# Sample attention in groups of four sequences on four column groups

## The reference, cut to what matters

```python
# prompt, per head: causal softmax over 256 positions
s_own = jnp.einsum('qhd,khd->qhk', q, k_own) * ATTN_SCALE
# sample, per sequence: 4 queries against 256 cached keys and its own new ones
kseq = jnp.concatenate([pool_k[pages].reshape(past, h, dh), kn, zeros], axis=0)
vseq = jnp.concatenate([pool_v[pages].reshape(past, h, dh), vn, zeros], axis=0)
# layer B: three groups (window, dilation) (128,1), (512,4), (2048,16), then
w = jax.nn.softmax(jnp.stack(lses, axis=0), axis=0)
o = jnp.sum(w[..., None] * jnp.stack(outs, axis=0), axis=0)
```

## Time and profile before

| | us |
|---|---|
| median of 3 runs (1825.51 to 1825.96) | 1825.53 |
| the profiled execution | 1829.23 |
| its span, first to last instruction | 1827.2 |
| attention A, 126.5 to 262.7 | 136.2 |
| attention B, 611.3 to 710.2 | 98.9 |

### The profile page before, as it was taken

One profiled execution on the slowest core, in us unless ns is written; L12 is line 12 of the kernel. 1 busy time (PEld: TensorE's weight loads), 2 busy tenths in 40 slices (PEclk: granted clock), 3 DMA queues, 4 the chain that ended last, 5 costly groups with the idle time before them and its releaser, 6 DMA issues.

```text
span 1827.2 us, 24864 instructions
## 1 busy us (share of the span) xinstructions
PE 1735.5 (95%) x9086; PEld 1434.3 (78%) x9086; DVE 1362.0 (75%) x1721; ACT 1038.8 (57%) x1043; POOL 56.1 (3%) x81
## 2 busy tenths in 40 slices
PE   7999989999989898589999999999999999999998
PEld 6876779999978677477877877877878878878776
DVE  5863426655577683788898888897888888988987
ACT  5433324443354241456776766776767767767765
POOL 0001101000000110100000000000000000000000
PEclk9998869999999897599999999999999999999999
DMA  9345414544643420188998998998998989989985
GB/s 327 116 154 175 139 46 135 165 141 122 201 156 116 141 105 24 47 277 321 362 336 326 356 344 321 359 334 328 354 346 324 355 312 361 345 322 360 335 326 200
DMA packets 232981, 452.97 MB, mean 248 GB/s; under 512 B 7584, under 2 KB 79264, under 8 KB 232784
## 3 DMA queue, kind: packets, MB, share of 16 engines
q1 hardware_dynamic: 224656, 421.93, 65.6%
q0 software_dynamic: 8256, 30.12, 5.0%
HBM read 447.30 MB, written 4.72 MB: 247 GB/s over the span
## 4 chain that ended last, share of the span: by engine, by line
PE 86%; DVE 8%; ACT 3%; issue 1%; DMA 1%; DVEq 0%; POOLq 0%; SPq 0%; ACTq 0%
PE psum L241 23%; PE psum L243 23%; PE psum L242 23%; PE psum L538 3%; PE psum L599 3%; PE psum L753 2%; PE psum L737 2%; DVE wlo L237 1%; PE psum L773 1%; PE psum L555 1%; ACT whi L233 1%; PE psum L580 1%; DVE rs L1150 1%; PE psum L521 1%; PE psum L476 1%
## 5 line engine op out<-in xcount | busy, mean ns | idle before, releaser
L237 DVE TENSOR_TENSOR wlo<-raw,whi 128x2048 fp32r<-128x2048 f32 (+1 forms) x404 | 911.5, 2261 | 227.6 <-ACT whi L233 227.5
L233 ACT ACTIVATE whi<-raw 128x2048 fp32r<-128x2048 f32 (+1 forms) x404 | 764.9, 1896 | 321.6 <-PE psum L243 321.5
L241 PE MATMUL psum<-whi,xgh 128*128 128x512 f32 x896 | 360.4, 402 | 7.7 <-DVE wlo L237 6.3
L243 PE MATMUL psum<-whi,xgl 128*128 128x512 f32 x896 | 356.4, 398 | 0.0
L242 PE MATMUL psum<-wlo,xgh 128*128 128x512 f32 x896 | 354.7, 396 | 0.0
L241 PE MATMUL psum<-hh,whi 128*128 128x288 f32 x800 | 246.1, 308 | 14.0 <-DVE hl L1294 9.1
L243 PE MATMUL psum<-hh,wlo 128*128 128x288 f32 x800 | 240.0, 300 | 0.0
L242 PE MATMUL psum<-hl,whi 128*128 128x288 f32 x800 | 239.1, 299 | 0.0
L241 PEld LDWEIGHTS psum<-whi,xgh 128*128 128x128 f32 x896 | 169.4, 189 | 49.0 <-DVE wlo L237 6.7
L243 PEld LDWEIGHTS psum<-whi,xgl 128*128 128x128 f32 x896 | 169.2, 189 | 41.2
L242 PEld LDWEIGHTS psum<-wlo,xgh 128*128 128x128 f32 x896 | 169.5, 189 | 39.6
(11 more groups left out here) (293 smaller groups left out, 1776.3 us busy)
## 6 DMA issues: line engine op xcount, KB each, us to landing
raw<-in_w_gu_moe SPq DMA_DIRECT2D x226, 1024.0 KB, 5.1
raw<-in_w_down_moe SPq DMA_DIRECT2D x112, 1024.0 KB, 5.0
raw<-in_w_gu_dense SPq DMA_DIRECT2D x22, 1024.0 KB, 5.1
raw<-in_w_qkv_a SPq DMA_DIRECT2D x12, 1024.0 KB, 12.5
raw<-in_w_down_dense SPq DMA_DIRECT2D x16, 704.0 KB, 4.6
kraw_a<-in_cache_a_k POOLq DMA_DIRECT2D x16, 512.0 KB, 4.6
vraw_a<-in_cache_a_v POOLq DMA_DIRECT2D x16, 512.0 KB, 4.9
raw<-in_w_q_b SPq DMA_DIRECT2D x6, 1024.0 KB, 5.1
```

The lines of the kernel that those rows point to most:

```text
L233: nc.scalar.activation(whi[:, p % SPL, 0:size], raw[:, p % RAW, 0:size], ACT.Copy).then_inc(hi_ready, 1)
L237: nc.vector.tensor_tensor(wlo[:, p % SPL, 0:size], raw[:, p % RAW, 0:size], whi[:, p % SPL, 0:size].bitcast(F32), ALU.subtract).then_inc(p ...
L241: nc.tensor.matmul(out, lh, rh, start=start, stop=False)
L243: return nc.tensor.matmul(out, ll, rh, start=False, stop=stop)
```

## The change

Each layer's attention becomes ten jobs in the order `JOBS`: eight prompt units ("p") and two groups of four sample sequences ("s"), and three more steps to finish. The transposes of the cached keys are laid out over the steps by `FILLS` (which sequences' keys in which step).

- Scores of a group: for each sequence and each of the four column groups, one matmul with 32 stationary columns (a pair of heads, 8 real columns in a band that belongs to that sequence) writes 32 rows of a tile of 128 rows (4 pairs x 4 sequences x 2 heads x 4 queries). Four sequences accumulate into one tile. In A there are two tiles (two groups of four pairs), in B one for each dilation group.
- Softmax: the maximum, `exp` and the sum run over a whole tile of 128 rows. The division by the sum comes after the values, as a scale of ACT's copy (`scale_out`).
- Values: the transposed probabilities (32 columns) are stationary and 128 value columns move; the new tokens come first, as one matmul of 512 moving columns for each pair. Of the 128x512 result, the diagonal blocks are wanted: `pick_rows` gets them by matmuls with slices of the identity, between `scale_out` (ACT) and `sample_out` (DVE).
- Loads: keys come one page at a time into a ring of 3 (A) or 6 (B) pages; transposed keys have 2 (A) or 4 (B) places. The values still have two places, and the load for sequence `q` waits for `spv_done` of `q - 2`.
- Gone: `sample_scores`, `turn_sample`, the old `sample_values` and L628.

Cut to its core (the lines that are left out are the matching buffers, masks, the DVE list and the removed code):

```diff
+JOBS = [("p", 0), ("p", 1), ("p", 2), ("s", 0), ("p", 3), ("p", 4), ("p", 5), ("p", 6), ("s", 1), ("p", 7)]
+FILLS = [(0,), (1, 2), (3,), (4,), (5,), (), (), (6, 7)]
...
+            def value_pages(b, q):
+                tg = b["tag"]
+                if q >= 2:
+                    eng.wait_ge(sem(f"spv_done_{tg}"), q - 1)
+                if b is A:
+                    for j in range(2):
+                        pg = eng.value_load(pgt[0:1, 2 * q + j:2 * q + j + 1], min_val=0, max_val=NPHYS - 1)
+                        eng.dma_start(b["vraw"][:, q % 2, j, :], io["cache_a_v"][0][bass.ds(pg, 1), :, :].rearrange("a p n -> p (a n)"))\
+                            .then_inc(sem(f"vraw_loaded_{tg}{q % 2}"), 16)
+                else:
+                    eng.dma_start(b["vraw"][:, q % 2], io["cache_b_v"][q].rearrange("(j p) n -> p j n", p=P)).then_inc(sem(f"vraw_loaded_{tg}{q % 2}"), 32)
...
+            def caches(b, first):
+                for pgi in range(first, 6):
+                    key_page(b, pgi)
+                eng.wait_ge(sem(f"kv_stored_{b['tag']}"), 64)
+                value_pages(b, 0)
+                value_pages(b, 1)
+                for pgi in range(6, 12):
+                    key_page(b, pgi)
+                for q in (2, 3):
+                    value_pages(b, q)
+                for pgi in range(12, 16):
+                    key_page(b, pgi)
+                for q in range(4, NSEQ):
+                    value_pages(b, q)
...
+                def sample_scores_a(q):
+                    keys_ready(q)
+                    if q == 4:
+                        eng.wait_ge(sem(f"so_copied_{tg}"), hp)
+                    s = q % 4
+                    for x in range(hp):
+                        for c in range(4):
+                            j = 4 * x + c
+                            ins = nc.tensor.matmul(ps[sbank + x][32 * c:32 * c + 32, 0:T], b["qblk"][:, s * b["qrow"] + 32 * j:s * b["qrow"] + 32 * j + 32],
+                                                   b["keys"][:, q % b["kb"], j, :], start=s == 0, stop=s == 3)
                     ins.then_inc(sem(f"sscored_{tg}"), 1)
...
+                def sample_scores_b(k, gr):
+                    eng.wait_ge(sem(f"exped_{tg}"), exped_count(b, k - 1))
+                    keys_ready(4 * gr + 3)
+                    for g in range(ng):
+                        for s in range(4):
+                            for c in range(nj):
+                                at_ = (4 * g + s) * b["qrow"] + 32 * c
+                                ins = nc.tensor.matmul(ps[b["score_banks"][g]][32 * c:32 * c + 32, 0:T], b["qblk"][:, at_:at_ + 32],
+                                                       b["keys"][:, s, c, :], start=s == 0, stop=s == 3)
+                        ins.then_inc(sem(f"sscored_{tg}"), 1)
...
+                def sample_values(k, gr):
+                    eng.wait_ge(sem(f"pt_copied_{tg}"), (k + 1) * hp)
+                    if ng > 1 and gr == 1:
+                        eng.wait_ge(sem(f"so_copied_{tg}"), hp)
+                    for x in range(hp):
+                        for c in range(4):
+                            new = b["vtok"][0:NSAMP, 2, (4 * x + c) * P:(4 * x + c + 1) * P].unsqueeze(1).to_broadcast([NSAMP, 4, P])
+                            nc.tensor.matmul(ps[sbank + x][32 * c:32 * c + 32, :].rearrange("p (s n) -> p s n", s=4),
+                                             b["spt"][0:NSAMP, x, 2 * P + 32 * c:2 * P + 32 * c + 32], new, start=True, stop=False)
+                    for s in range(4):
+                        q = 4 * gr + s
+                        eng.wait_ge(sem(f"vraw_loaded_{tg}{q % 2}"), 32 * (q // 2 + 1))
+                        for x in range(hp):
+                            for half in range(2):
+                                for c in range(4):
+                                    j = 4 * x + c
+                                    ins = nc.tensor.matmul(ps[sbank + x][32 * c:32 * c + 32, s * P:(s + 1) * P],
+                                                           b["spt"][:, x, half * P + 32 * c:half * P + 32 * c + 32],
+                                                           b["vraw"][:, q % 2, half, j * P:(j + 1) * P], start=False, stop=s == 3 and half == 1)
+                        ins.then_inc(sem(f"spv_done_{tg}"), 1)
...
+                def pick_rows(gr, x):
+                    eng.wait_ge(sem(f"so_scaled_{tg}"), gr * hp + x + 1)
+                    for s in range(4):
+                        for r in range(2):
+                            ins = nc.tensor.matmul(ps[sbank + x][64 * r:64 * r + 64, 16 * s:16 * s + 16], b["pvs"][:, s * P + 64 * r:s * P + 64 * r + 64],
+                                                   pick[:, s, r], start=True, stop=True)
+                    ins.then_inc(sem(f"picked_{tg}"), 1)
...
+                for t in range(len(JOBS) + 3):
+                    fills = slot_fills(b, t)
+                    kind, u = JOBS[t] if t < len(JOBS) else ("", 0)
+                    done, du = JOBS[t - 1] if 1 <= t <= len(JOBS) else ("", 0)
+                    if kind == "p":
+                        scores(t, u)
+                    elif kind == "s" and ng > 1:
+                        sample_scores_b(t, u)
+                    for n in fills[0:2]:
+                        turn_keys(n)
+                    if done:
+                        turn_probs(t - 1, 0)
+                    if ng == 1:
+                        for q in ((), (0,), (1,), (2, 3), (), (), (), (4, 5), (6, 7))[t] if t < 9 else ():
+                            sample_scores_a(q)
+                    for n in fills[2:]:
+                        turn_keys(n)
+                    if done and hp == 2:
+                        turn_probs(t - 1, 1)
+                    if t >= 2 and t - 2 < len(JOBS) and JOBS[t - 2][0] == "s":
+                        sample_values(t - 2, JOBS[t - 2][1])
+                    if done == "p":
+                        values(t - 1, du)
+                    if t >= 3 and t - 3 < len(JOBS) and JOBS[t - 3][0] == "s":
+                        for x in range(hp):
+                            pick_rows(JOBS[t - 3][1], x)
...
+                def scale_out(gr, x):
+                    eng.wait_ge(sem(f"spv_done_{tg}"), 4 * (gr + 1))
+                    if x == 1:
+                        eng.wait_ge(sem(f"picked_{tg}"), gr * hp + 1)
+                    nc.scalar.activation(b["pvs"][:, :], ps[b["s_bank"] + x][:, :], ACT.Copy, scale=b["sst"][:, gr, 8 + x:9 + x])\
+                        .then_inc(sem(f"so_scaled_{tg}"), 1)
...
+                for t in range(len(JOBS) + 3):
+                    fills = [n for n in slot_fills(b, t) if n % 2 == 0]
+                    done, du = JOBS[t - 1] if 1 <= t <= len(JOBS) else ("", 0)
+                    for n in fills[0:1]:
+                        copy_keys(n)
+                    if done:
+                        copy_probs(t - 1, 0)
+                    for n in fills[1:]:
+                        copy_keys(n)
+                    if t < len(JOBS):
                         for x in range(hp):
+                            exp(t, x)
+                    if done and hp == 2:
+                        copy_probs(t - 1, 1)
+                    if done == "p" and (du * hp + hp - 1) % 2 == 1:
+                        h = du * hp + hp - 1
+                        eng.wait_ge(sem(f"pv_done_{tg}"), du + 1)
+                        nc.scalar.activation(b["oT"][:, h // 2, 0:SEQ], ps[b["pv_bank"]][:, 0:SEQ], ACT.Copy).then_inc(sem(f"o_copied_{tg}"), 1)
+                    if t >= 3 and t - 3 < len(JOBS) and JOBS[t - 3][0] == "s":
+                        for x in range(hp):
+                            scale_out(JOBS[t - 3][1], x)
...
```

More of the change, by code:

```diff
@@ L160, in build_program, with slot_fills @@
+        def slot_fills(b, t):
+            return [n for q in (FILLS[t] if t < len(FILLS) else ()) for n in range(2 * b["fills"] * q, 2 * b["fills"] * (q + 1))]
         A["dest"] = [A["qT"][:, i] for i in range(8)] + [A["kT"][:, i] for i in range(8)]
@@ L387, in norm_add @@
+            for pgi in range(3):
+                key_page(A, pgi)
+            store(A, io["ak"], io["av"])
+            caches(A, 3)
             def norm_add(tag, before):
@@ L651, in _ @@
             to_tokens(A)
[L652 removed]
+            attend(A)
             residual(P_WO, tiles_wo, KD, "wo", "o_split_a", hh2, hl2)
@@ L1164, in attend @@
             def attend(b):
-                tg, nj, ng, hp, kr, hq, rows = b["tag"], b["nj"], b["ng"], b["hp"], b["kr"], b["hq"], b["rows"]
-                two = len(b["kt_banks"]) == 2
-                chain(V.memset(b["qblk"][:, :, :], 0.0))
-                V.tensor_copy(b["keys"][:, :, PAST:PAST + NSAMP], b["kT"][:, :, SEQ:T]).then_inc(sem(f"new_keys_{tg}"), 1)
+                tg, nj, ng, hp = b["tag"], b["nj"], b["ng"], b["hp"]
+                for i in range(b["kb"]):
+                    ins = V.tensor_copy(b["keys"][:, i, :, PAST:T], b["kT"][:, :, SEQ:T])
```

(35 more changed lines are left out.)

447 lines of the change are left out of this document (166 added, 281 removed).

## The result

The changed kernel took 1832.47 us (median of five, 1831.77 to 1834.65), the kernel before 1825.51: ratio 1.0042, 95% interval 1.0029 to 1.0056. Compared once more later, with twelve executions, it was 1.0018 [1.0004, 1.0032]. So it is slower, by 0.2 to 0.4%; the forecast was 1829.5, which is 4.0 above the kernel before, and the two comparisons have 7.0 and 3.5 by their medians. The profiled execution took 1832.47 with a span of 1830.8, against 1827.2 before.

The account below looks back on a forecast made before the run. The prediction took PE to bound the kernel (86% of the span ends on it). A gaining 7.3 us and B losing 11 gave net +4: profiled 1829.2 becomes 1833, less 3.7 to the median, 1829.5; range 1809 to 1843.

Parts of the forecast that it names:

- What goes from PE: PE in both attentions: sets of four column-group matmuls replace sample scores and values; A's PE falls from 127 to about 65 us.
- slot walk: Both attentions, durations summed slot by slot from the first exp to the split: A 122.4 us, B 100.4 us.
- Rival 3: Column groups' weight loads in both attentions don't overlap running matmuls: +10 us, 1839; chance 0.06.
- The loop between the engines: Prompt slots of both attentions: scores, maximum, exp, probabilities and handovers take 6.1 us a slot, 7.3 or 7 at half clock.
- The value waits: Each group's third sequence's values load late; PE waits about 6 then 1.5 us in A, 4 in B, twice per layer.
- The slots: Eleven slots in each attention, priced one by one: A gains 7.3 us, B loses 11.
- The clock: PE in both attentions at half clock in slots 1 and 2, after value waits, in tails; full clock worth 11 and 7 us.
- Rival 1: PE's clock returns soon after each wait; A gains 18, B loses 4: 14 us faster, 1811.5; chance 0.28.
- The signs: Expected in the trace: A gaps 5 to 7 us, B about 4, prompt slots 6 to 7, B above 98.9, clock below 0.80.
- the waits don't cost: Value loads in both attentions: third sequence's copies land early, so no wait is paid; some 15 us faster; chance 0.03.

Follow-up runs that it names:

- late_values: Changed kernel with group value matmuls cut in two, ScalarE's probability copy ahead of exponentials, and sequences 6 and 7's values loaded where cached keys were: 1782.94 us, 0.9751.

## Why the prediction was right, and where it was not

The forecast was 1829.5, slower at 0.46; measured 1832.5 and 1830.5. Its steps:

- **What goes from PE.** The 65 us of PE that A was to fall to do not come out of their own terms: 127 less 43 and 30, plus 25 for the new sets, is 79. The slot walk did not use them. Busy time times granted clock says 62 to 63 us for the new A at full clock; without value waits it was busy 74.1 at 0.85 granted, and in late_values 70.1 at 0.89. The price of a set was right: a set of four with 288 columns was put at 0.5 us in a stream and 1.0 at half clock, and 6.03 over twelve is 0.50. Rival 3 is out, and more clearly than its price says: a weight load of 32 columns (PEld at L578) shows as 0.11 us and not the 0.03 I took, so eight in a row without overlap would be 0.88 us a set, more than the whole set takes. With it goes the rule in the Trainium skill ("TensorE: Matmul & The Clock Gate", Part 3, What overlaps and what doesn't) that weight loads hide only behind another row group, as far as this form goes.
- **The loop between the engines.** 6.1 us a prompt slot was a little long: 169.38 to 174.51 in A is 5.1, 646.17 to 651.78 in B 5.6 (first scores to next first scores, at full clock).
- **The value waits.** Place and cause right, and the size nearly. The third sequence was to come 7.2 us (A) and 4.5 (B) after the first's were used; it came 7.0 (180.37 to 187.36) and 4.3 (657.75 to 662.04) after. PE waited 5.3 and then 1.4 us in A's first group, for 6 and 1.5. In B the sum had one wait of 4 in each group and none for the fourth sequence; they were 3.5 and 1.4 us in the first group, 3.5 and 0.6 in the second. In all PE stood still 22.4 us in them (13.6 and 8.8), for 23.
- **The slots.** The walk of A had the scores of slots 4 to 7 and 9 at 166.9, 172.5, 191.5, 203.9 and 225.0; they were at 169.4, 174.5, 194.2, 204.8 and 225.5, and the split at 257.5 instead of 255.4: slot 4 came 2.5 us late, slot 6 took 1.7 less, the end behind slot 9's scores 1.6 more. A gained 5.2 of the 7.3. B's walk was 3.4 us too long: its first `exp` ended 1.9 us earlier after the first scores than I had it, slot 5 with the value waits took 15.3 us and not 13.0, and slot 8 8.1 and not 10.3, because its twelve sets found the clock full. B lost 7.7 of 11. That the sum came out at +2.4 in the stages against +4 is partly luck: errors of 2 us with both signs stand in it, 1.2 us outside the stages were put at nothing, and the same new A can be 8 us shorter in another execution.
- **The clock.** Half clock for slots 1 and 2, behind the value waits and in the tails: 0.71 and 0.70 granted, so the sign and the places were right. Rival 1 failed at its condition, a clock that is soon back: from 616 PE was busy 8.00 of 8 us at 0.55, and behind B's first value wait it was still 0.50 from 664 to 680, with PE busy 14.5 of 16 us. The size stays open. Full clock throughout was put at 11 and 7 us of the stages' length, and no run has it; without the value waits busy time alone fell by 3.5 to 14.1 in A and by 5.1 to 6.0 in B, at 0.85 and 0.78.
  The short warm-up of the Trainium skill (Part 1 of the same page, The HAM clock gate), which would have made it 1819 to 1820, does not show here either; the trace agrees with its other half, that an idle TensorE loses the clock.
- **The signs.** The two stages' lengths, the lower clock and A's two gaps came as named; B's gaps were 3.5 us and the prompt slots 5.1 and 5.6, a little under what was named.
- **What I did not see.** The clock and the waits are one cost and not two. I gave "the waits don't cost" 15 us, where my own waits in the sum are 23, and counted the clock beside them. Taken away, the waits were worth 37 to 39. And I took the stage's length as one number, where the same code of A takes 122.6 to 130.9.

So the change's own mechanism works, in both stages. What it lacked was cover for four loads, and the second half of each group one slot later turns +0.3% into -1.6%.

## What to carry to other kernels

When a change takes work off the bounding engine, ask what each load was hidden behind: work that is batched by four with two buffers waits for its third load, however fast the batch is. Read a stage as busy plus idle time at a fixed number of instructions; if the busy time changes, it is the clock, and a microsecond of idle time taken away can be worth nearly two. Take more than one profile before you read a busy time that way. Buffers that another phase has finished with are often the cheapest way to start a load early.

## What the runs showed of the hardware

- A wait can cost twice on TensorE: once as idle time, and again as matmuls at half clock behind it. With the value waits taken away (no_value_wait) the median fell by 37 to 39 us, and 19 to 21 of them were idle time; the busy time of the two stages fell by 9 to 20 us, by which profile of the new code is taken beside it.
- The granted clock of the same instruction list differs between executions, 0.71, 0.77 and 0.81 in A, worth 10.6 us of busy time. A comparison of one profile each can have the sign wrong: changed against before is +3.6 us in one pair of spans and -0.5 in the other (1826.7 against 1827.2).
- 68 float32 matmuls of no use in the two stages raised the granted clock from 0.71 and 0.70 to 0.88 and 0.87, and the kernel did not get longer.
- Four column groups with the same rows run side by side in float32: 0.50 us for four matmuls of 32 by 288, weight loads included.
- GpSimd issues one cached page with its table lookup each 1.14 us; four in a row put 4.5 us in front of a landing of 5.7.
